# A depthwise convolution accumulated in PSUM instead of SBUF, with its chunk loop written out

## The reference

```python
def conv_module(xn, hist, w_in, b_in, w_dw, b_dw, ln_g, ln_b, w_out, b_out):
    h = xn @ w_in + b_in
    a, gate = jnp.split(h, 2, axis=-1)
    u = a * jax.nn.sigmoid(gate)
    upad = jnp.concatenate([hist.astype(u.dtype), u], axis=1)
    y = lax.conv_general_dilated(            # depthwise, 31 taps, one filter per feature
        upad, w_dw[:, None, :], window_strides=(1,), padding='VALID',
        dimension_numbers=('NWC', 'WIO', 'NWC'), feature_group_count=u.shape[-1]) + b_dw
    y = jax.nn.silu(layernorm(y, ln_g, ln_b))
    out = y @ w_out + b_out
    return out, upad[:, -CONV_HIST:]
```

## Time and profile before

| what | value |
|---|---|
| time, median of 3 runs | 3474.57 us (3445.11 to 3509.44) |
| span of the profiled execution | 3441.0 us |
| lowest timed run, beside that span | 3445.11 us |
| convolution stage, first gate product to last chunk's sum | about 86 to 528 us |
| busy over the whole span | PE 86%, DVE 39%, ACT 29%, POOL 28% |

### The profile page before, as it was taken

How to read it: one execution, slowest core, us unless ns; L and a number is a source line. 1 busy time by engine, 2 the same in 40 slices (tenths; PEclk the granted TensorE clock), 3 DMA queues, 4 the chain that set the end, 5 groups by cost and what they waited for, 6 DMA issues and landing times.

```text
span 3441.0 us, 49665 instructions
## 1 busy us (share of the span) xinstructions
PE 2972.1 (86%) x17970; PEld 2775.7 (81%) x17970; DVE 1332.7 (39%) x2005; ACT 994.2 (29%) x1549; POOL 971.2 (28%) x436
## 2 busy tenths in 40 slices
PE   5535336999999999989999999899898999999998
PEld 4535335889999999979997777778797999999997
DVE  6999996421111111251113555555334111111114
ACT  4323225232111111221113544455423211111113
POOL 2757571222212121231110000055613122222221
PEclk9767667999999999999996999988789999999998
DMA  3000000111111111122411201377511111111111
GB/s 95 19 24 12 24 12 20 43 37 40 52 40 46 43 43 49 37 68 82 121 39 31 70 25 25 101 254 262 195 43 37 40 46 43 40 52 34 52 36 70
DMA packets 243747, 206.54 MB, mean 60 GB/s; under 512 B 18252, under 2 KB 218956, under 8 KB 243652
## 3 DMA queue, kind: packets, MB, share of 16 engines
q1 hardware_dynamic: 230535, 186.66, 17.8%
q10 hardware_dynamic: 13133, 18.80, 1.6%
HBM read 183.16 MB, written 23.13 MB: 60 GB/s over the span
## 4 chain that ended last, share of the span: by engine, by line
PE 72%; DVE 15%; issue 7%; ACT 3%; DMA 1%; POOL 1%; DVEq 0%; ACTq 0%; SPq 0%; POOLq 0%
PE PS L706 19%; PE PS L708 18%; PE PS L707 18%; DVE yacc L1644 8%; PE PS L964 4%; PE PS L990 3%; PE PS L948 2%; DVE tm L1506 2%; PE PS L1027 1%; DVE rs L1485 1%; PE PS L1068 1%; PE PS L1040 1%; PE PS L1069 1%; PE PS L1041 1%; ACT pr L1394 1%
## 5 line engine op out<-in xcount | busy, mean ns | idle before, releaser
L706 PE MATMUL PS<-xhi,whi 128*128 128x352 f32 x3456 | 1144.4, 331 | 269.0 <-DVE u L1608 188.3
L708 PE MATMUL PS<-xlo,whi 128*128 128x352 f32 x3456 | 1122.3, 325 | 0.0
L707 PE MATMUL PS<-xhi,wlo 128*128 128x352 f32 x3456 | 1121.0, 324 | 0.0
L622 POOL TENSOR_TENSOR wlo<-wraw,whi 128x1024 fp32r<-128x1024 f32 x208 | 510.7, 2456 | 1608.4 <-ACT whi L1136 1608.4
L706 PEld LDWEIGHTS PS<-xhi,whi 128*128 128x128 f32 x3456 | 657.5, 190 | 311.6 <-DVE u L1608 190.3
L707 PEld LDWEIGHTS PS<-xhi,wlo 128*128 128x128 f32 x3456 | 660.9, 191 | 0.0
L708 PEld LDWEIGHTS PS<-xlo,whi 128*128 128x128 f32 x3456 | 658.6, 191 | 0.0
L1543 DVE TENSOR_TENSOR ht<-PS,ht 128x352 f32<-128x352 f32 x132 | 69.1, 525 | 908.4 <-PE PS L708 904.4
L1136 ACT ACTIVATE whi<-wraw 128x1024 fp32r<-128x1024 f32 x208 | 218.8, 1052 | 595.2 <-PE PS L708 567.2
L706 PE MATMUL PS<-hhi,whi 128*128 128x352 f32 x1056 | 341.2, 323 | 8.8 <-issue 8.8
L707 PE MATMUL PS<-hhi,wlo 128*128 128x352 f32 x1056 | 338.5, 321 | 0.0
(11 more groups left out here) (197 smaller groups left out, 3036.5 us busy)
## 6 DMA issues: line engine op xcount, KB each, us to landing
wraw<-in_ffn_w_gu SPq DMA_DIRECT2D x88, 512.0 KB, 3.8
kr<-in_cache_k SPq DMA_DIRECT2D x64, 512.0 KB, 4.8
vr<-in_cache_v SPq DMA_DIRECT2D x64, 512.0 KB, 4.8
wraw<-in_ffn_w_down SPq DMA_DIRECT2D x32, 384.0 KB, 3.4
wraw<-in_attn_w_in SPq DMA_DIRECT2D x24, 512.0 KB, 3.9
wraw<-in_ffn_w_down SPq DMA_DIRECT2D x32, 320.0 KB, 3.1
wraw<-in_conv_w_in SPq DMA_DIRECT2D x16, 512.0 KB, 3.8
wraw<-in_conv_w_out SPq DMA_DIRECT2D x8, 512.0 KB, 4.0
```

The lines of the kernel that those rows point to most:

```text
L622: nc.gpsimd.tensor_tensor(wlo[:, s, :], wraw[:, s, :], whi[:, s, :].bitcast(F32), ALU.subtract).then_inc(w_lo, 1)
L706: nc.tensor.matmul(out, wh, hi[:, k, blk(b)], start=(k == 0), stop=False)
L707: nc.tensor.matmul(out, wl, hi[:, k, blk(b)], start=False, stop=False)
L708: m = nc.tensor.matmul(out, wh, lo[:, k, blk(b)], start=False, stop=(k == kc - 1))
```

## The change

- The accumulator `yacc` is no longer an SBUF tile but PSUM banks 6 and 7, 1024 fp32 columns. The instructions that read and write it stay what they were: one input is `u` in SBUF, the other and the output are now in PSUM.
- KP goes from 11 to 12: ACT makes 12 products a chunk and POOL 11 additions; DVE keeps 19 taps, so 18 instructions of the accumulating kind.
- The sample part on DVE becomes one multiply of 128x992 over overlapping windows (new L1634) instead of four of 128x248, the sum (new L1643) stays, and the bias addition goes to ACT (new L1263, signalled by `s_bias`, for which PE waits before the layer-norm sums).
- The copy of the parameters to `wc` is gone, since the chunk loop is written out and reads `par` directly. The copy of the history goes to ACT (`history`, new L1235), as do the two saves of the tails (new L1257, L1258).
- The loops over chunks on DVE, ACT and POOL are written out instead of run as hardware loops; PE's is not.

```diff
         ys = at("ys", [P, C, NS], F32, after("uprod"))
...
+        yacc = PS[:, 6:8, :].rearrange("p a f -> p (a f)")
...
-        KP = 11
+        KP = 12
...
-            with pool.Fori(0, C) as c:
+            for c in range(C):
                 low_parts(c + 1)
...
                     pool.wait_ge(a_tap, c * KP + (i + 1))
                     if i > 1:
                         pool.wait_ge(p_tap, c * (KP - 1) + (i - 1))
-                    pool.nop(nofuse=True)
+                    elif c > 0:
+                        pool.wait_ge(c_done, c)
...
+            def history(q):
+
+                if q == 0:
+                    act.wait_ge(s_ev0, 5)
+                else:
+                    act.wait_ge(s_prod, q)
+                nc.scalar.activation(us[:, :, 0:HIST], hist[:, q, :].rearrange("p (b t) -> p b t", t=HIST),
+                                     ACT.Copy).then_inc(u_hist, 1)
+
             def glu(q):
                 next_hi(q, 0)
...
+                    if i == 2:
+                        nc.scalar.activation(utail[:, q, 0:HIST], u[:, SEQ:SEQ + HIST], ACT.Copy)
+                        nc.scalar.activation(utail[:, q, HIST:HIST + NS].rearrange("p (b t) -> p b t", t=TNEW),
+                                             us[:, :, HIST:HSEG], ACT.Copy).then_inc(u_tail, 1)
+                if q + 1 < C:
+                    history(q + 1)
+                act.wait_ge(s_red, q + 1)
+                nc.scalar.activation(ycv[:, q, SEQ:T], ys[:, q, :], ACT.Identity,
+                                     bias=par[:, q, R_BDW:R_BDW + 1]).then_inc(s_bias, 1)
+
+            history(0)
+            for q in range(C):
                 glu(q)
...
-            with dve.Fori(0, C) as c:
+            for c in range(C):
+                w = par[:, c, :]
+                if c > 0:
+                    dve.wait_ge(u_tail, c)
...
+                dve.wait_ge(u_hist, c + 1)
+                nc.vector.tensor_tensor(
+                    up, windows, par[:, c, R_DW:R_DW + KW].rearrange("p (a b k) -> p a b k", a=1, b=1).broadcast_to(
+                        [P, NREQ, TNEW, KW]), ALU.mult).then_inc(s_prod, 1)
+                nc.vector.tensor_scalar(yacc, u[:, 0:SEQ], w[:, R_DW:R_DW + 1], w[:, R_BDW:R_BDW + 1],
+                                        ALU.mult, ALU.add).then_inc(cv, 1)
                 for k in range(1, KD):
...
+                    dve.wait_ge(cv, tapped)
+                    nc.vector.scalar_tensor_tensor(yacc, u[:, k:k + SEQ], w[:, R_DW + k:R_DW + k + 1], yacc,
+                                                   ALU.mult, ALU.add).then_inc(cv, 1)
```

More of the change, by code:

```diff
@@ L134, in hybrid_step @@
         uprod = at("uprod", [P, NREQ * TNEW, KW], F32, after("u"))
-        yacc = at("yacc", [P, SEQ], F32, after("uprod"))
-        ys = at("ys", [P, NS], F32, after("yacc"))
+        ys = at("ys", [P, C, NS], F32, after("uprod"))
         prods = at("prods", [P, 3, SEQ], F32, where["ssq"][0])
@@ L142, in hybrid_step @@
         hist = at("hist", [P, C, NREQ * HIST], F32, after("ht"))
-        wc = at("wc", [P, NPAR], F32, after("hist"))
-        utail = at("utail", [P, C, HIST + NS], F32, after("wc"))
+        utail = at("utail", [P, C, HIST + NS], F32, after("hist"))
         ustate = at("ustate", [HIST + NS, D], F32, where["xlo"][0])
@@ L267, in hybrid_step @@
         c_done = sem("c_done")
+        u_hist = sem("u_hist")
+        u_tail = sem("u_tail")
+        s_prod = sem("s_prod")
+        s_red = sem("s_red")
+        s_bias = sem("s_bias")
         st_tr = sem("st_tr")
@@ L358, in hybrid_step @@
         HR = NREQ * HIST // 2
-        KP = 11
+        KP = 12
         KD = KW - KP
-        KCH = KD + TNEW + 7
         def blk(b):
@@ L817, in _ @@
                 for b in range(NB):
+                    if b == NB - 1:
+                        pe.wait_ge(s_bias, c + 1)
                     m = nc.tensor.matmul(PS[:, b, 0:BW], ones[:, :], ycv[:, c, blk(b)],
@@ L1225, in glu @@
                     act.wait_ge(mm[1], q * NB + (b + 1))
-                    if not isinstance(q, int) or q > 0:
+                    if q > 0:
                         act.wait_ge(ev[0], seen(0, q - 1, b))
-                    act.nop(nofuse=True)
                     nc.scalar.activation(ht[:, b, :], PS[:, NB + b, 0:BW], ACT.Sigmoid,
-                                         bias=par[:, ds(q, 1), R_BIN + 1:R_BIN + 2].rearrange("p a b -> p (a b)")
-                                         ).then_inc(gate, 1)
+                                         bias=par[:, q, R_BIN + 1:R_BIN + 2]).then_inc(gate, 1)
                 next_hi(q, 1)
@@ L1238, in glu @@
                     past(act, p_tap, q * (KP - 1) + (max(i - 3, 1) if i >= 3 else 0))
-                    act.nop(nofuse=True)
                     k = KD + i
                     nc.scalar.activation(prods[:, i % 3, :], u[:, k:k + SEQ], ACT.Copy,
-                                         scale=wc[:, R_DW + k:R_DW + k + 1]).then_inc(a_tap, 1)
-            glu(0)
-            with act.Fori(1, C) as q:
+                                         scale=par[:, q, R_DW + k:R_DW + k + 1]).then_inc(a_tap, 1)
+                    if i == 2:
[9 more added lines that the diff above has]
+            for q in range(C):
                 glu(q)
@@ L1586, in _ @@
             us = u[:, US0:ULEN].rearrange("p (b t) -> p b t", t=HSEG)
+            u_all = u[:, US0:ULEN]
+            windows = bass.AP(tensor=u_all.tensor, offset=u_all.offset,
+                              ap=[list(u_all.ap[0]), [HSEG, NREQ], [1, TNEW], [1, KW]])
             up = uprod[:, :, :].rearrange("p (b t) k -> p b t k", t=TNEW)
-            with dve.Fori(0, C) as c:
[L1589 to L1603, removed]
+            tapped = 1
+            for c in range(C):
+                w = par[:, c, :]
+                if c > 0:
+                    dve.wait_ge(u_tail, c)
                 for b in range(NB):
@@ L1619, in _ @@
                 dve.wait_ge(ev[0], c * NB + NB)
[L1621 to L1627, removed]
@@ L1628, in _ @@
-                for k in range(1, KD):
[L1629 to L1645, removed]
@@ L1646, in _ @@
-                stepped(n[0])
+                dve.wait_ge(u_hist, c + 1)
[4 more added lines that the diff above has]
+                                        ALU.mult, ALU.add).then_inc(cv, 1)
+                tapped += 1
@@ new lines, in _ @@
+                for k in range(1, KD):
+                    if k == 2:
+                        dve.wait_ge(s_prod, c + 1)
+                        nc.vector.tensor_reduce(ys[:, c, :], uprod[:, :, :], AX.X, ALU.add).then_inc(s_red, 1)
+                    dve.wait_ge(cv, tapped)
+                    nc.vector.scalar_tensor_tensor(yacc, u[:, k:k + SEQ], w[:, R_DW + k:R_DW + k + 1], yacc,
+                                                   ALU.mult, ALU.add).then_inc(cv, 1)
+                    tapped += 1
@@ L1648, in _ @@
+                dve.wait_ge(cv, tapped)
                 dve.wait_ge(p_tap, c * (KP - 1) + (KP - 1))
[L1649 to L1653, removed]
+                nc.vector.tensor_tensor(ycv[:, c, 0:SEQ], yacc, yp[:, :], ALU.add).then_inc(c_done, 1)
             dve.wait_ge(st_tr, 1)
```

6 lines of the change are left out of this document (3 added, 3 removed).

## The result

The changed kernel takes 3311.34 us, the median of four runs (3276.58 to 3315.39), against 3475.27 (3445.11 to 3509.44) for the kernel before, also four. The ratio is 0.956, with a 95% interval of 0.951 to 0.961: some 153 us less, 136 to 170. Medians and ranges in this text are of all executions, while the ratios and their intervals leave out single ones over 1.5% longer than the fastest of their kernel, as 3509.44 is here. The profiled execution has a span of 3313.3 us where the one before had 3441.0; its own time is 3315.02.

A forecast was written before the change was run, and what follows sets the result against it. DVE was taken to bound the convolution stage, taking turns with POOL over SBUF. Savings of 150.2 us over seven chunks and 18.4 in chunk 0, together 168.6, took 3474.57 to 3306.0; range 3264 to 3360.

The forecast's parts named there:

- The lower end of the range, 3264: Whole kernel: POOL's additions at 2.38 (9 us less) and run scatter, lowest 29 under the median.
- What bounded before: turns of DVE and POOL over SBUF: Convolution stage: two-SBUF-input DVE instructions alternate with POOL, costing 134 us in L1644 and about 35 in L1632.
- 1.32 us for an accumulation in PSUM: DVE's 18 accumulations a chunk: 1.32 us each with wait, 23.8 us together; bounds 1.32 and 2.39.
- two and three cycles a column: Rivals for PSUM accumulation: two cycles, 2.39 us each, 3446 us, chance 0.05; three, 3.4 us, 3591 us, chance 0.02.
- Tap 0 into PSUM 1.28 us: DVE's first tap of a chunk: 1.28 us into PSUM, as L1852, in place of 0.81.
- POOL's addition 2.54 us apart when undisturbed: POOL, each chunk: eleven additions at 2.54, 27.9 us; rival of 3.15 each, 3360 us, chance 0.08.
- The large multiply waits for the second low part: DVE's 992-column multiply, 1.19 us, meets the second of POOL's two 2.38 us low parts and waits until T+4.8.
- T+6.0: Start of POOL's first addition, T being the end of its last addition; T+5.6 before the multiply pushes it.
- The bound passes to POOL, DVE 1.4 us earlier: Chunk period: POOL ends at T+33.8, DVE at T+32.4; 33.8 us for 55.26, 150.2 us less over seven chunks.
- Chunk 0: First chunk: closing sum at 121.7 instead of 140.11, 18.4 us less, about 3 us given away by ACT's order.
- Sum 168.6 us: Total saving: 150.2 from seven chunk periods plus 18.4 from chunk 0.
- Behind the last closing sum nothing changes: After the convolution stage: the rest, PE's products from 530 us on, stays untouched.

The follow-up runs named there:

- the two kernels with input and output apart: Changed kernel with accumulations reading PSUM and writing an SBUF scratch tile (3315.89 us), or reading an SBUF tile and writing PSUM (3469.50 us).
- KP = 11: Changed kernel with one tap moved back from ACT and POOL to DVE; 3289.98 us, ratio 0.945 to the kernel before.
- KP = 13: Changed kernel with one more tap moved to ACT and POOL; 3312.28 us, ratio 0.952 to the kernel before.
- PSUM alone: Kernel before with only the accumulator yacc moved to PSUM banks 6 and 7; 3320.14 us, ratio 0.953.
- PSUM undone: Changed kernel with yacc an SBUF tile again, all else kept; 3451.07 us, ratio 0.998 to the kernel before.
- two SBUF inputs: Changed kernel whose accumulations read u and an SBUF tile holding tap 0 and write PSUM, leaving the accumulating out; 3469.50 us, one execution.
- scratch output: Changed kernel whose 18 accumulations a chunk read the PSUM accumulator and write an SBUF scratch tile; 3315.89 us, one execution.
- history later: Changed kernel with ACT's history copy of chunk 0 moved behind that chunk's sigmoids and high parts; 3308.01 us, one run.
- better version: Changed kernel with 11 ACT taps, chunk 0's history copy behind its sigmoids, and tap 0 ahead of the large multiply; 3286.59 us, ratio 0.944.

## Why the prediction was right, point by point

The forecast was 3306.0 us, the median is 3311.34; the range held. That the two are only 5 us apart is in part luck: the four executions spread over 38.8 us, the attention stage alone differed by 44.5 between the two profiles, and the forecast knew nothing of that. What carries the prediction is the stage, 168.6 us forecast and 172.3 measured. (The lower end of the range, 3264, does not come out of its own terms: 3306.0 less 9 and less 29 is 3268.) By its own steps:

- **What bounded before: turns of DVE and POOL over SBUF.** Right, and settled by the two kernels with input and output apart. The rows of L1821 and L1637 had pointed to it: one SBUF input, never slowed. The sentence that all the slow instructions read two SBUF inputs holds for those that it names, but passes over L1639, which reads one and took 2.31 us. It changed nothing in the sum, since the change moves that bias to ACT (0.31 us there).
- **1.32 us for an accumulation in PSUM.** Right: 1.277 to 1.291 with the next one 0.03 behind. The 144 rows of L1645 exclude two and three cycles a column, as the row of 128 columns, L1784, had suggested. Nor does one PSUM input lengthen the closing sum, 1225 ns before and after.
- **Tap 0 into PSUM 1.28 us**: 1.335.
- **POOL's addition 2.54 us apart when undisturbed**: 2.55, with durations of 2.40. The spacing was the right number to sum; by the durations (2.38) the sum would have come out for DVE as the bound, 1.2 us a chunk lower. Perfetto Trace Analysis of the Trainium skill, section GPSIMD Engine Instruction, had recommended the spacing, and these rows agree.
- **The large multiply waits for the second low part**: right, 2.73 us for 1.19. I had it push POOL's first addition to T+6.0; the addition starts at T+5.2 (126.59 for 121.36) and is only 0.3 us longer than the others (2.71). That is the 0.5 us by which the period, 33.8 forecast and 33.30 measured, was too long.
- **The bound passes to POOL, DVE 1.4 us earlier**: 1.66 to 1.69 in five of the seven chunks behind chunk 0, 1.97 and 1.21 in the other two, and KP = 11 and KP = 13 move the last closing sum the way this says.
- **Chunk 0**: first gate product forecast near 88.5, seen at 88.50; closing sum 121.7, seen at 121.47. The price of the history copy was put at 3 us; the run with it moved says 4.6, because the collision of the multiply with the second low part goes too.
- **Sum 168.6 us**: the stage gives 172.3. Of the 3.7 us between them 3.5 are 7 x 0.5.
- **"Behind the last closing sum nothing changes"**: for the work this holds to 0.1 us (2534.8 and 2534.9), but the term left out the clock of the attention stage, which took 44.5 us back in the profiled execution. The lowest run of the changed kernel, 3276.58, is 38.4 under the profiled one; its mean granted clock was 0.944, that of the other three 0.932 to 0.934. The means, 3465.2 without the 3509.44 and 3303.7, differ by 161.6 us; the medians, 3475.27 and 3311.34, differ by 164, and the ratio's centre gives 153. All three lie under the 172.3 of the stage; the unprofiled executions show no stages, so how much of that is the clock is not known. With four runs each the interval (136 to 170) does not separate the forecast 168.6 from the measured centre.

What was not tried: the share of the written-out loop apart from that of the single multiply in the 4.0 us a chunk that PSUM alone does not give. They were only measured together, beside the twelfth tap.

## What to carry to other kernels

When two engines are both slow on shapes that are fast elsewhere, compare minimum and maximum of a single line, and then ask which operands the lines that vary have and the steady lines lack. Here it was the second SBUF input of a DVE instruction beside POOL, and moving one operand to PSUM gave 17.9 of the 22.0 us that a chunk became shorter, while the rest of the change without it gave 1.4. Before moving work between engines, work out the period of each engine with the contention taken out: the balance of 11 or 12 taps, the place of the one instruction that still has two SBUF inputs, and one copy queued too early on ACT were together worth another 20 us.

Compare two versions by the stage that was changed, start to end, and not by the spans alone, if another stage's clock differs between executions.

## What the runs showed of the hardware that I had not expected

- The prompt's attention stage has one of several lengths for the same instructions: 379.3 us (kernel before, PSUM undone, KP = 13), 413.7 and 413.8 (KP = 11, two SBUF inputs), 423.8 or 423.9 (changed kernel, scratch output, history later, better version) and 447.5 us (PSUM alone). The granted clock goes with it in all ten profiles: its mean over the stage is 0.92, 0.83, 0.81 and 0.75 for the four lengths, with DVE busy 196 us and ACT 177 to 178 each time. What decides on the stretches at the lower clock is open; no run was made on it.
- A write to PSUM costs `tensor_scalar` its faster pace: 807 ns from SBUF to SBUF, 1335 ns from SBUF to PSUM for the same 1024 columns. For the accumulation the place of the operands makes 9 ns at most when POOL is idle or not in its way: 1285 ns in SBUF, 1290 in PSUM, 1281 from PSUM to SBUF.
- Two instructions that collide both show it in their durations: the accumulation 3.24 us for 1.29 and POOL's addition 3.15 for 2.40, some 3.3 us for a pair that would take 2.55 side by side.
- A `tensor_scalar` from SBUF to SBUF meets POOL too, with a single SBUF input: 2.31 us for 32 columns, where a copy of 32 columns with POOL idle has 0.18, and 2.88 for 0.81 at 1024 columns. The same instruction into PSUM had 1334 to 1342 ns in all eight chunks.
